# A two-layer transformer block pair on one core: convolution columns in one product for both parts of the rows, eight heads in one group

## What is computed

```python
u = rms_norm(h, mix_pre_g[l])
(a_b, a_c, a_x, b_u, c_q, c_k, c_v, d_q, d_k, d_v, d_f, gate_logits) = _split(u @ w_in[l], IN_SPLITS)
y_a = short_conv_mixer(a_b, a_c, a_x, ...)      # (a_b * conv3(a_c * a_x)) @ w
y_b = conformer_conv_mixer(b_u, ...)            # silu(layer_norm(conv31(a * sigmoid(g)))) @ w
y_c = diff_attention_mixer(c_q, c_k, c_v, ...)  # 4 heads, 2 softmaxes each, causal
y_d = forgetting_attention_mixer(d_q, d_k, d_v, d_f, ...)  # 8 heads, decay from a running sum
merged = g0 * y_a + g1 * y_b + g2 * y_c + g3 * y_d
h = h + rms_norm(merged @ w_o[l], mix_post_g[l])
```

## Time and profile before

| | us |
|---|---|
| median of 3 executions (1622.06 to 1623.53) | 1623.16 |
| the profiled execution, its own time | 1625.09 |
| its span, first to last instruction | 1623.3 |
| mixing of layer 0, slots 2 to 46 | 211.6 to 484.4 |
| mixing of layer 1, the same | 892.5 to 1165.5 |

### The profile page before, as it was taken

How to read it: one execution, slowest core, us unless ns; L and a number is a source line. 1 busy time by engine, 2 the same in 40 slices (tenths; PEclk the granted TensorE clock), 3 DMA queues, 4 the chain that set the end, 5 groups by cost and what they waited for, 6 DMA issues and landing times.

```text
span 1623.3 us, 22333 instructions
## 1 busy us (share of the span) xinstructions
PE 1601.5 (99%) x9203; PEld 1384.1 (85%) x9203; DVE 1180.7 (73%) x1335; ACT 809.6 (50%) x1064; POOL 35.1 (2%) x60
## 2 busy tenths in 40 slices
PE   8999999999999999999999999999999999999998
PEld 7888899987888888888888999878888888888886
DVE  5766667899856766676667689997677666786785
ACT  5444444555545534454345445555454444775773
POOL 0000000000000000000000000000000000000100
PEclk9999999999999999999999999999999999999999
DMA  8555554454555554465555644545565554523521
GB/s 321 185 186 201 184 212 178 169 190 138 178 190 201 188 199 182 164 234 195 192 183 182 232 170 167 182 154 180 186 222 187 184 201 141 186 107 111 195 104 53
DMA packets 55910, 292.75 MB, mean 180 GB/s; under 512 B 5872, under 2 KB 10368, under 8 KB 29696
## 3 DMA queue, kind: packets, MB, share of 16 engines
q1 hardware_dynamic: 52464, 279.47, 48.5%
q10 hardware_dynamic: 3344, 11.85, 2.0%
HBM read 290.23 MB, written 1.06 MB: 179 GB/s over the span
## 4 chain that ended last, share of the span: by engine, by line
PE 81%; DVE 11%; DVEq 3%; ACT 2%; issue 1%; DMA 1%; POOL 0%; ACTq 0%; SPq 0%; POOLq 0%
PE ps L1633 18%; PE ps L1610 15%; PE ps L1611 15%; PE ps L1612 15%; PE ps L1636 9%; DVE wlo L1062 4%; DVE mix L1269 2%; PE ps L2114 1%; PE ps L1723 1%; PE ps L1693 1%; PE ps L2125 1%; DVE small L1361 1%; PE ps L1694 1%; ACT tmp L714 1%; PE ps L1699 1%
## 5 line engine op out<-in xcount | busy, mean ns | idle before, releaser
L1062 DVE TENSOR_TENSOR wlo<-raw,whi 128x2048 fp32r<-128x2048 f32 (+3 forms) x267 | 596.2, 2241 | 128.0 <-ACT whi L711 120.5
L711 ACT ACTIVATE whi<-raw 128x2048 fp32r<-128x2048 f32 (+3 forms) x267 | 497.7, 1875 | 332.4 <-DMA raw<-stream 329.4
L1633 PE MATMUL ps<-xs,whi 128*128 128x512 f32 x1280 | 319.9, 392 | 0.0
L1633 PEld LDWEIGHTS ps<-xs,whi 128*128 128x128 f32 x1280 | 232.4, 189 | 43.1
L1610 PE MATMUL ps<-whi,yar 128*128 128x512 f32 x620 | 243.9, 393 | 0.9 <-ACT mix L981 0.9
L1611 PE MATMUL ps<-wlo,yar 128*128 128x512 f32 x620 | 241.4, 389 | 0.0
L1612 PE MATMUL ps<-whi,yar 128*128 128x512 f32 x620 | 241.0, 389 | 0.0
L1610 PE MATMUL ps<-xs,whi 128*128 128x256 f32 x704 | 202.0, 287 | 0.0
L1611 PE MATMUL ps<-xs,whi 128*128 128x256 f32 x704 | 199.1, 283 | 0.0
L1612 PE MATMUL ps<-xs,wlo 128*128 128x256 f32 x704 | 199.0, 283 | 0.0
L1636 PEld LDWEIGHTS ps<-xs,wlo 128*128 128x128 f32 x1280 | 174.6, 190 | 12.5
(11 more groups left out here) (235 smaller groups left out, 1594.5 us busy)
## 6 DMA issues: line engine op xcount, KB each, us to landing
raw<-stream SPq DMA_DIRECT2D x202, 1024.0 KB, 4.8
raw<-stream SPq DMA_DIRECT2D x102, 512.0 KB, 4.7
raw<-stream SPq DMA_DIRECT2D x22, 384.0 KB, 3.9
gpre<-pre_gain ACTq DMA_DIRECT2D x8, 512.0 KB, 4.1
gpost<-post_gain ACTq DMA_DIRECT2D x6, 512.0 KB, 5.2
mix<-cum ACTq DMA_DIRECT2D x2, 1024.0 KB, 7.1
raw<-stream SPq DMA_DIRECT2D x6, 256.0 KB, 6.9
raw<-stream SPq DMA_DIRECT2D x4, 320.0 KB, 4.1
```

The source lines that it names most:

```text
L711: A(whi[:, s, 0:w], raw[:, s, 0:w], ACT.Copy).then_inc(hi_ready, 1)
L1062: TT(wlo[:, s, 0:w], raw[:, s, 0:w], whi[:, s, 0:w].bitcast(F32), ALU.subtract).then_inc(lo_v, 1)
L1633: pe.matmul(bank(b).rearrange("p (a t) -> p a t", a=2), wh[:, k, m * P:(m + 1) * P], xs[:, :, k, :], start=(k == 0), stop=False)
```

## The change

Three things, and new numbers in `mix_steps`. (1) The ten convolution columns go through `both_parts`, into bank pairs 2 and 3 (even slots) or 0 and 1 (odd slots); DVE takes all ten with the `tensor_reduce`, so for columns 0, 1, 4, 5, 8, 9 ACT's copy is gone and for 2, 3, 6, 7 the sum comes ahead of the multiplication, which then reads SBUF. The tanh of columns 0 and 1 is now an own ACT step on SBUF, after a semaphore (`gate_sum_in`) from DVE. (2) The two groups of the first token half in each attention become one of eight score blocks (groups 0 and 5), so there are 6 groups, with the same products. (3) `f_turn` and `f_sum` use banks 6 and 7 in place of 2 and 3, and f_sum moves from slot 12 into slot 17.

```diff
-GROUPS1 = 8
+GROUPS1 = 6
-COLS_V = (2, 3, 6, 7)
+COLS_V = (0, 2, 1, 3, 4, 5, 6, 7, 8, 9)
...
-        score1 = ps[:, 4:6, :].rearrange("p m (i k) -> p i m k", i=2)
+        def score1(t):
+            return ps[:, 4:6, :].rearrange("p m (i k) -> p i m k", i=4 - 2 * t)
+
+        def prob1(t):
+            return prob[:, :, :] if t else prob[:, :, :].rearrange("p e (a k) -> p (e a) k", a=2)
...
         def group1(g):
-            w, hp = g // 4, g % 2
-            return w, (g % 4 // 2 if w == 0 else 1 - g % 4 // 2), hp
+
+            if g in (0, 5):
+                return g // 3, 0, (0, 1)
+            return g // 3, 1, ((g + 1) % 2,)
...
-                        elif i in (0, 1):
-                            chunk_used(act, c)
-                            A(gate_b[:, 2 * i:2 * i + 2, :].rearrange("p m t -> p (m t)"), src, ACT.Tanh,
-                              scale=0.5).then_inc(evac_a, 1)
...
-                            A(fbuf[0:16, 760:1016], src[0:16, 0:T], ACT.Copy).then_inc(evac_a, 1)
+                            A(fbuf[0:16, 760:1016], bank(2)[0:16, 0:T], ACT.Copy).then_inc(evac_a, 1)
...
+                    elif kind == "tanh":
+                        act.wait_ge(gate_sum_in, l * 2 + (n + 1))
+                        block = gate_b[:, 2 * n:2 * n + 2, :].rearrange("p m t -> p (m t)")
+                        A(block, block, ACT.Tanh, scale=0.5).then_inc(gate_th, 1)
...
-                        act.wait_ge(sc_done, l * 8 + 4)
+                        act.wait_ge(sc_done, l * GROUPS1 + 3)
...
+                taken = tmp[:, 0:512].rearrange("p (m t) -> p m t", m=2)
+
+                def both_added(out, b):
+                    return dve.tensor_reduce(out, ps[:, b:b + 2, :].rearrange("p m (a t) -> p m t a", a=2), AX, ALU.add)
...
-                        src = bank(p % 2)
-                        if i in (2, 3):
+                        b0 = 2 - p % 2 * 2
+                        chunk_used(dve, c)
+                        if i in (0, 1):
+                            both_added(gate_b[:, 2 * i:2 * i + 2, :], b0).then_inc(evac_v, 1)
+                            dve.drain()
+                            dve.sem_inc(gate_sum_in, 1)
+                        elif i in (4, 5):
+                            both_added(a_c[:, 2 * (i - 4):2 * (i - 4) + 2, :], b0).then_inc(evac_v, 1)
+                            dve.drain()
+                        elif i in (8, 9):
+                            both_added(a_b[:, 2 * (i - 8):2 * (i - 8) + 2, :], b0).then_inc(evac_v, 1)
+                            dve.drain()
+                        elif i in (2, 3):
                             j = i - 2
-                            chunk_used(dve, c)
-                            cols_taken(dve, l, j)
+                            both_added(taken, b0).then_inc(evac_v, 1)
+                            dve.drain()
+                            dve.wait_ge(gate_th, l * 2 + (j + 1))
                             STT(out=pad_b[:, 2 * j:2 * j + 2, B_CONV - 1:PB], in0=gate_b[:, 2 * j:2 * j + 2, :],
-                                scalar=1.0, in1=src.rearrange("p (m t) -> p m t", m=2), op0=ALU.add,
-                                op1=ALU.mult).then_inc(evac_v, 1)
+                                scalar=1.0, in1=taken, op0=ALU.add, op1=ALU.mult)
                             dve.drain()
-                        elif i in (6, 7):
+                        else:
                             j = i - 6
-                            chunk_used(dve, c)
-                            cols_taken(dve, l, 4 + j)
-                            TT(pad_a[:, 2 * j:2 * j + 2, A_CONV - 1:PA], a_c[:, 2 * j:2 * j + 2, :],
-                               src.rearrange("p (m t) -> p m t", m=2), ALU.mult).then_inc(evac_v, 1)
+                            both_added(taken, b0).then_inc(evac_v, 1)
+                            dve.drain()
+                            TT(pad_a[:, 2 * j:2 * j + 2, A_CONV - 1:PA], a_c[:, 2 * j:2 * j + 2, :], taken, ALU.mult)
                             dve.drain()
                     elif kind == "out":
                         b, half = n // 2, n % 2
@@ -1283,7 +1300,6 @@
                                 STT(out=acc_a[:, m, :], in0=v, scalar=w, in1=acc_a[:, m, :], op0=ALU.mult, op1=ALU.add)
                         dve.drain()
                         if tap == A_CONV - 1:
-                            cols_taken(dve, l, 9)
                             TT(acc_a, acc_a, a_b, ALU.mult).then_inc(mixa_done, 1)
                     elif kind == "a_split":
                         dve.wait_ge(ahi_done, l + 1)
@@ -1317,7 +1333,7 @@
...
+                            for i in range(ne // 2) if t else (slice(0, 4),):
+                                if t:
+                                    head = 4 * hps[0] + 2 * i
+                                    TT(pb[:, 2 * i:2 * i + 2, :], score1(t)[:, i], decay[:, head:head + 2, :], ALU.add)
+                                else:
+                                    TT(pb.rearrange("p (i m) k -> p i m k", m=2), score1(t),
+                                       decay[:, :, 0:P].rearrange("p (i m) k -> p i m k", m=2), ALU.add)
                         dve.drain()
-                        dve.tensor_reduce(sm[:, 8:12], prob[:, :, 0:nk], AX, ALU.max)
...
+                        if i in (0, 2, 1, 3, 4, 5, 6, 7, 8, 9):
+                            if p == 3:
+                                cols_taken(pe, l, COLS[part])
+                            elif p > 3 and part == 0:
+                                cols_taken(pe, l, COLS[p - 2])
+                            both_parts(c, 2 - p % 2 * 2 + part, part)
+                            continue
                         if part == 0:
-                            cols_taken(pe, l, COLS[p - 2])
...
-                        if t == 0 and j == 0:
-                            pe.wait_ge(f_ready, l + 1)
...
+                            pe.wait_ge(f_ready, l + 1)
                         turned = steps_before(MIX_PE, (kind, n), "flip")
-                        if turned and w == 1 and t == 1:
+                        if turned and w == 1:
```

More of the change, by code:

```diff
@@ L193, in mix_steps @@
             pe.append((slot + 0.5 + half / 20, kind, (n, half)))
-    at(pe, (9.5264,), "f_turn")
-    at(pe, (12.02,), "f_sum")
+    at(pe, (8.025,), "f_turn")
+    at(pe, (17.5167,), "f_sum")
     at(pe, (35.02,), "ln_stats")
-    at(pe, (37.12,), "ln_back")
-    at(pe, (17.02, 19.04, 21.04, 23.04, 25.06, 27.04, 28.0489, 30.3752), "scores")
-    at(pe, (19.02, 21.2526, 23.02, 25.0491, 27.1998, 29.02, 31.02, 33.5205), "turn")
-    at(pe, (20.04, 22.04, 24.04, 26.04, 28.04, 30.04, 32.04, 34.2328), "values")
+    at(pe, (36.525,), "ln_back")
@@ L214, in mix_steps @@
+    at(act, (1.192, 1.5, 7.75, 14.0829, 14.5, 14.525, 17.3766, 19.035, 19.366, 19.5, 20.5, 22.5), "take", COLS_TAKEN)
+    at(act, (2.5, 5.1739), "tanh")
+    at(act, (25.0571, 28.785, 32.1452, 33.5, 37.2167, 37.8833, 42.5, 46.5793), "gate")
+    at(act, (13.8165,), "f_log")
+    at(act, (18.2033,), "f_store")
+    at(act, (23.6724,), "f_load")
     at(act, (15.08,), "a_split")
-    at(act, (17.02, 19.04, 21.04, 23.9947, 25.06, 27.04, 29.04, 31.04), "scores")
-    at(act, (19.02, 21.02, 23.02, 25.04, 27.02, 29.02, 31.02, 33.02), "turn")
@@ L233, in mix_steps @@
-    at(dve, (9.02,), "f_turn")
-    at(dve, (10.06,), "f_tok")
-    at(dve, (12.12,), "f_sum")
-    at(dve, (25.02, 28.1), "f_mask", (1, 0))
-    at(dve, (15.8129, 18.0313, 21.04, 23.04, 25.06, 27.04, 29.04, 31.04), "scores")
-    at(dve, (18.02, 20.02, 22.0574, 24.02, 26.02, 27.82, 29.82, 32.02), "weigh")
-    at(dve, (20.04, 22.0561, 24.04, 26.04, 28.05, 30.05, 32.05, 34.03), "values")
-    at(dve, (27.1, 27.9403), "o_scale")
-    at(dve, (28.08, 30.08), "o_split")
+    at(act, (40.1889,), "ln_back")
@@ new lines, in mix_steps @@
+    at(act, (40.8695,), "ln_split")
+    at(act, (45.55,), "m_turn")
+    at(dve, (2.5157, 2.55, 2.689, 2.891, 3.55, 4.55, 5.55, 5.7454, 8.55, 9.55, 10.3386, 11.65, 12.55, 13.55, 14.55,
+             15.55, 16.55, 17.1927, 18.55, 19.55, 22.0568, 22.5487, 23.045, 23.05, 24.55, 26.7067, 28.0674, 28.55,
+             29.4478, 30.55, 31.0601, 32.0761, 33.55, 35.03, 35.545, 36.05, 37.05, 37.5318, 40.3328, 40.4151, 42.55,
+             42.9198, 43.3, 43.8339, 45.285, 45.55, 46.5681), "split")
+    at(dve, (2.6, 2.6445, 5.025, 5.5, 5.9407, 8.5, 10.4193, 10.5, 11.5, 12.5), "take", COLS_V)
@@ new lines, in mix_steps @@
+    at(dve, (27.352, 29.7639, 32.0592, 35.2925, 37.5, 42.6424, 44.427, 46.6324), "out")
+    at(dve, (5.52, 5.54, 6.1361, 7.4508, 11, 11.25, 12.525, 13.05, 14.6325, 14.7151, 14.8801, 14.9627, 15.0452,
+             17.4785, 17.7642, 18.05, 20.0371, 20.0541, 20.57, 25.256, 25.452, 25.648, 27.508, 30.174, 30.268,
+             30.362, 31.3801, 31.7, 32.0931, 32.11, 33.05), "conv")
+    at(dve, (10.75, 11.575, 14.06), "a_conv")
+    at(dve, (19.785,), "a_split")
+    at(dve, (7.9754,), "f_turn")
+    at(dve, (14.7976,), "f_tok")
@@ L242, in mix_steps @@
```

(13 more changed lines are left out.)

225 lines of the change are left out of this document (100 added, 125 removed).

## The result

| | before | after |
|---|---|---|
| median us (lowest to highest, executions) | 1623.35 (1622.06 to 1623.97, 6) | **1611.72** (1611.53 to 1612.03, 6) |
| profiled execution, its span | 1625.09, 1623.3 | 1612.03, 1610.2 |
| mean granted clock over the span | 0.998 | 1.000 |

The ratio is 0.993, 95% interval 0.992 to 0.994: faster by 11.6 us. The forecast was 1616.8 and the range 1613.0 to 1622.5. The sign was right. The size was not: nearly twice the gain came, and it lies outside the range.

The account below looks back on a forecast made before the run. PE, at 99% busy, was taken as the bound. Product -3.8, waits -2.6, visits -0.8, narrow places +0.8 sum to -6.4 us against the profiled 1625.09: 1618.7, forecast median 1616.8 us, range 1613.0 to 1622.5.

Parts of the forecast that it names:

- Sum in mixing: Both layers' mixing stages: product, waits and visits saved, narrow places added, -6.4 us in all.
- The product: Ten convolution columns per layer in 512-column products on PE: 20 chunks at 0.19 us, 3.8 us saved.
- The waits: PE's waits at scores 0 (for ACT) and turn 5 (for o_split) become hidden: 2.6 us saved.
- The visits: PE leaves the chunk stream 18 times per layer, not 22; 0.08 us each and per change to scores: 0.8 us saved.
- visits twice as dear: Allowance in the range's lower end, 1613.0: PE's visits save a further 0.8 us.
- The narrow places: Take 1, take 6 and turn 0, where DVE barely keeps up with PE: 0.8 us added over two layers.
- take 6: DVE's reduction of convolution column 6, due at 24.5 us when PE wants its bank at 24.5: margin none.
- turn 0: PE's turn 0 wants weigh 0, done at 25.2 us; PE gets there at 25.8: margin 0.6 us.
- DVE's bill: DVE per layer, column 3's chunk end to last tap: takes +9.1, larger groups give back 2, net +7.1 us.
- the 8.0 us of waiting for ACT's part: DVE's idle time per layer ahead of splits, which takes or taps were to fill.
- Room at the last tap: DVE's margin at the convolution's last tap before PE's ln_stats: 3.0 us, where it was 5.0.
- DVE becomes the bound: Rival, column 3's take to ln_stats: takes wait for PE with splits behind them; slower, median 1630 us; chance 0.12.

Follow-up runs that it names:

- b1: Kernel before with scores 0 moved into column 16 on PE and o_split 0 ahead of split 26 on DVE: 1623.50 us, ratio 0.9999.
- b4: Kernel before with larger groups alone, turn 0, values 0 and scores 5 later, plus the moves of scores 0 and o_split 0: 1619.23 us, ratio 0.9974.
- d1: New kernel with idle DVE reductions before the last tap, one in layer 0, three in layer 1: layer 0 grows by 0.46 us, layer 1 by 4.37.
- a1: Kernel before with the product alone (ten columns through both_parts), old groups and old order of the rest: 1638.22 us, ratio 1.0091.
- a3: New kernel with each 512-column product of the ten columns made as two of 256: 1616.36 us, ratio to before 0.9956.
- a2: Kernel before with the groups alone (6 per layer), old products, old order but for steps that fall away: 1627.75 us, ratio 1.0024.

## Why the prediction was right or wrong

- **Sum in mixing: -6.4 forecast, -10.2 found**; over the run 11.6 by the medians.
- **The product**: 3.8 forecast, 3.46 by the run that undoes it. Right, the row of the same form in the feed-forward carried over to 0.02 us per chunk.
- **The waits**: 2.6 forecast, by the list of waits, and both kinds are gone from that list; 3.2 by the starts. Right as a size, wrong as a reason. I took each wait by itself and said it is hidden where it goes; on the kernel before the same moves give nothing. That they count only since DVE does its work in time is how I read b1 and b4; no run shows it by itself. I also misread one move: turn 4 comes half a chunk *sooner* than turn 5 did, not 2.7 us later; its wait is gone since DVE does o_split 0 ahead of a split.
- **The visits: the step that failed.** "0.08 each, and going over to the 64-row products of scores costs about as much ahead of them": 0.8 us, where the traces show 3.4. I priced the visit from the earlier trace rows, a visit of full-sized products, which is the cheap kind (0.03), and put all of it on the count of visits. The half-sized kind costs 0.41, and the new groups make fewer changes to it: by these prices 1.3 of the 1.67 us per layer, the rest is open. Half of the miss, 2.6 of 5.1 us, is this one term. Its bound was "visits twice as dear"; the row for the other kind, the start after a 64-row visit, was in the trace and I did not take it.
- **The narrow places**: +0.8 allowed, nothing came. Two of the three places were rightly picked: take 6 is where the product alone loses 7 us per layer, and turn 0 where it loses next. In the new order both are narrow and hold, in layer 0: take 6 is done at 257.13 us and PE wants its banks at 257.79, 0.7 us of room where I had none; weigh 0 is done at 317.40 and turn 0 starts at 318.44, 1.0 where I had 0.6.
- **DVE's bill**: +7.1 over the stretch forecast, from which I gave "about 10" for the stage; it is +12 in the stage and +10.8 per layer over the run. That did not hurt, since the 8.0 us of waiting for ACT's part were filled, as the first part of the forecast has it. Room at the last tap 2.4 against 3.0. The forecast asked only whether the tap is in time; the split behind it has 1.0 us, and it is what PE meets first (d1).
- **"DVE becomes the bound"** had the right mechanism, and a1 shows it, with the fall of the clock on top that I had not priced: 1638, where the rival said 1630. It was the case of half the change, not of the whole.
- **Outside mixing**: nothing forecast, about 1.4 us by the medians (11.6 - 10.2), which is no credit to the change. A wait of 0.9 us in the second hybrid layer for ACT is in the first trace and not in the new one, but it is in a3's (1.1), and the kernel before has it at 0.6 in its second trace. Why it comes and goes is open.
- The parts do not add: product alone +14.9, groups alone +4.4, the two moves alone +0.1, all with the new orders -11.6 (medians against 1623.35; against the kernel before beside each run it is +14.7, +4.3 and -0.4). The gain is of the combination. That larger groups relieve DVE, that the order puts takes ahead of splits and taps where DVE has nothing else, and that PE's savings stay savings only so is how I read it: product and groups together in the old order, and the whole new order on the old work, were not run.

## What to carry to other kernels

Price a visit of PE to another kind of product by the kind: find in the trace one visit of each form, and count how often the form changes, not how often the stream is left. Where one engine is at 99% and a second one, in order, feeds it at 80% (DVE in mixing, 219.5 of 272.8 us), a wait taken from the first can come back at the next hand-over, as in b1; so test parts together as well as alone. And price a wait on PE above its length, since the granted clock may fall with it: 1.5 us came on top in d1, and in a1 PE had 6 us of work at half the clock behind a wait of 6.7; but in the traced execution of a2, waits of 1.4 and 2.2 us brought no fall.

## What I had not expected of the hardware

- After PE waited 1.2 and 1.1 us within four microseconds (d1) the granted clock was 0.50 for some 3 us; in a wait of 6.7 us (a1) it fell, and it was at or near 0.50 for most of 10 us, 6 of them behind the wait. The new kernel has no such wait in mixing and is at 1.00 in all of it.
- A visit of 64-row products costs 0.41 us beyond its products, one of products of 64 columns 0.4, one of full-sized turns 0.03; half-sized kinds next to each other share the cost (2.08 against 2.40 us for the same products).
- A product of 512 columns in place of two of 256 with the same weights saves 0.011 us.
